# Attention in the first pass: values as weights in two column halves, output by feature, softmax division ahead of the transposes

## The reference, cut to what matters

```python
logits = jnp.where(valid[:, None, :], logits + bias, NEG_INF)
sink = jnp.broadcast_to(sinks.astype(jnp.float32).reshape(1, ATT_KV_HEADS, ATT_GROUP, 1, 1, 1), logits.shape[:-1] + (1,))
probs = jax.nn.softmax(jnp.concatenate([logits, sink], axis=-1), axis=-1)[..., :KEY_BAND]
out = jnp.einsum('bhgcqk,bckhd->bcqhgd', probs, vb)
y = jnp.concatenate([y_rwkv.astype(h.dtype), y_att], axis=-1) @ w_out[l]
```

## Time and profile before

| | |
|---|---|
| median of 3 runs | 2862.46 us (2858.02 to 2865.93) |
| the profiled execution's own time | 2862.2 us |
| its span, first to last instruction | 2860.2 us |
| TensorE matmul / weight load busy | 2483.3 us / 1604.6 us |
| VectorE / ScalarE / GpSimd busy | 1079.2 / 733.6 / 406.3 us |
| mean granted TensorE clock | 0.931 |

### The profile page before, as it was taken

One profiled execution on the slowest core, in us unless ns is written; L12 is line 12 of the kernel. 1 busy time (PEld: TensorE's weight loads), 2 busy tenths in 40 slices (PEclk: granted clock), 3 DMA queues, 4 the chain that ended last, 5 costly groups with the idle time before them and its releaser, 6 DMA issues. The chain is left out here.

```text
span 2860.2 us, 68640 instructions
## 1 busy us (share of the span) xinstructions
PE 2483.3 (87%) x28334; PEld 1604.6 (56%) x28335; DVE 1079.2 (38%) x2622; ACT 733.6 (26%) x1782; POOL 406.3 (14%) x455
## 2 busy tenths in 40 slices
PE   3999999999997699999999995589999999989800
PEld 1888888888886567777777773323333333323200
DVE  0344544545445245656565554211111111111118
ACT  0244343443443113222222221012222222212200
POOL 0212112121121011212121210000000000000013
PEclk7999999999997899999999996599999999999955
DMA  8011121121123823232323210745535679999597
GB/s 318 8 68 66 45 88 47 45 89 45 45 82 121 335 80 108 103 123 83 126 91 113 91 69 37 320 180 220 220 132 220 268 270 362 349 426 358 204 369 284
DMA packets 59767, 472.50 MB, mean 165 GB/s; under 512 B 8284, under 2 KB 9344, under 8 KB 38944
## 3 DMA queue, kind: packets, MB, share of 16 engines
q1 hardware_dynamic: 39432, 403.49, 36.3%
q0 software_dynamic: 9936, 36.18, 3.6%
q10 hardware_dynamic: 10184, 29.67, 2.7%
HBM read 373.90 MB, written 95.42 MB: 164 GB/s over the span
## 5 line engine op out<-in xcount | busy, mean ns | idle before, releaser
L1726 PE MATMUL ps<-arena 128*32 128x512 f32 x4608 | 516.4, 605 | 35.2 <-DMA arena<-wex 35.2
L452 PE MATMUL ps<-arena 128*128 128x128 f32 (+2 forms) x3584 | 419.7, 276 | 2.1 <-ACT arena L601 2.1
L452 PEld LDWEIGHTS ps<-arena 128*128 128x128 f32 (+2 forms) x3584 | 406.9, 186 | 17.0 <-ACT arena L601 13.0
L1726 PEld LDWEIGHTS ps<-arena 128*32 128x32 f32 x4608 | 151.3, 112 | 393.6 <-issue 366.7
L1107 PE MATMUL ps<-arena 64*64 64x64 f32 x8704 | 298.1, 222 | 30.4 <-ACT arena L1310 9.1
L1107 PEld LDWEIGHTS ps<-arena 64*64 64x64 f32 x8704 | 278.0, 136 | 59.1 <-issue 58.0
L1740 PE MATMUL ps<-arena 128*32 128x512 f32 x2304 | 263.8, 598 | 18.1 <-DMA arena<-wex 16.8
L1252 PE MATMUL ps<-arena 128*128 128x512 f32 x512 | 238.9, 610 | 0.7 <-ACT arena L1329 0.7
L1946 DVE TENSOR_TENSOR arena<-arena,ps 128x256 f32<-128x256 f32 x72 | 29.9, 415 | 456.3 <-ACT arena L1785 456.3
L1785 ACT ACT_TABLE_LOAD x36 | 46.2, 1283 | 603.8 <-PE ps L1726 603.8
L463 PE MATMUL ps<-arena 128*128 128x256 f32 (+1 forms) x512 | 174.3, 488 | 0.0
(11 more groups left out here) (321 smaller groups left out, 3033.3 us busy)
## 6 DMA issues: line engine op xcount, KB each, us to landing
arena<-wex SPq DMA_DIRECT2D x108, 2048.0 KB, 9.6
mid<-arena SPq DMA_DIRECT2D x16, 2568.0 KB, 8.5
arena<-mid SPq DMA_DIRECT2D x16, 2568.0 KB, 10.4
arena<-ada SPq DMA_DIRECT2D x12, 2048.0 KB, 11.6
y<-arena ACTq DMA_DIRECT2D x36, 512.0 KB, 8.0
arena<-x SPq DMA_DIRECT2D x31, 512.0 KB, 5.4
arena<-w_in SPq DMA_DIRECT2D x8, 1232.0 KB, 25.6
y<-arena SPq DMA_DIRECT2D x16, 512.0 KB, 11.3
```

What stands on the lines that cost most here:

```text
L452: mm = pe.matmul(bank[name][0:m, at:at + P], V["w_in"][:, kk, w0:w0 + m], V["hT"][:, kk, :], start=(kk == 0), stop=(kk == KD - 1))
L1726: mm = pe.matmul(bank[("HA", "HB")[g]][rows[j], :], xT[:, kk, rows[j]], slot[j][:, at:at + 2 * FH], start=(kk == 0), stop=(kk == KD - 1))
```

## The change

- The step `att5` on TensorE has the values as weights (64 columns) and the transposed probabilities streaming, two heads (256 columns) at a time. The first two heads of a group are written to rows 0 to 63 of C2, the other two to rows 64 to 127: rows are now features. It waits for both halves of `PT` before its first matmul.
- The softmax division moves: VectorE gets a step at the place of `exp_0` and `exp_1` in the order, which waits for `probs`, computes the reciprocal of the sums of 4 heads and multiplies the 4x192 probabilities in place; it signals `pn`, and the transposes wait for that.
- VectorE's `att5_1` is a plain copy of C2 into `ya`.
- In pass 2 the transposes of `ya` are gone; ScalarE copies `ya` straight into `yT` (signal `yaT`), and bank O1 loses its use "yT".
- The rows of `w_out` are reordered ahead of the launch, to match the new order of the attention output.

```diff
--- before.py
+++ after.py
@@ -551,7 +551,7 @@
 
             def att4(g):
                 def go(t, b):
-                    S.wait(pe, "probs", 2 * t + g + 1)
+                    S.wait(pe, "pn", 2 * t + g + 1)
                     for half, name in enumerate(("T0", "T1")):
                         B.wait_free(pe, name, f"P{g}", t)
                         for i in range(2):
@@ -564,12 +564,13 @@
             def att5(g):
                 def go(t, b):
                     B.wait_read(pe, "C2", "gate", t)
-                    for i in range(4):
-                        h = 4 * g + i
-                        B.wait_read(pe, f"T{i // 2}", f"P{g}", t)
-                        for part in range(2):
-                            v = V["qkv"][b if part else 1 - b][:, 640 + 64 * g:704 + 64 * g]
-                            mm = pe.matmul(bank["C2"][:, 64 * h:64 * h + 64], V["PT"][:, i, P * part:P * part + P], v,
+                    for half in range(2):
+                        B.wait_read(pe, f"T{half}", f"P{g}", t)
+                    for part in range(2):
+                        v = V["qkv"][b if part else 1 - b][:, 640 + 64 * g:704 + 64 * g]
+                        for half in range(2):
+                            mm = pe.matmul(split(bank["C2"][64 * half:64 * half + 64, 256 * g:256 * g + 256], 2), v,
+                                           V["PT"][:, 2 * half:2 * half + 2, P * part:P * part + P],
                                            start=(part == 0), stop=(part == 1))
                     mm.then_inc(S["pv"], 1)
                 return go
@@ -860,18 +861,26 @@
                     B.free(dve.tensor_copy(V["PT"][:, 2:4, :], split(bank["T1"][:, :], 2)), "T1")
                 return go
 
+            def probs(g):
+                def go(t, b):
+                    S.wait(dve, "probs", 2 * t + g + 1)
+                    g4 = slice(4 * g, 4 * g + 4)
+                    dve.tensor_tensor(V["den"][:, g4], V["sm"][:, g4], V["es"][:, g4], ALU.add)
+                    dve.drain()
+                    dve.reciprocal(V["den"][:, g4], V["den"][:, g4])
+                    dve.drain()
+                    keys = V["Pm_v"][:, :, 64:256]
+                    dve.tensor_tensor(keys, keys, per_channel(V["den"][:, g4], KEYS), ALU.mult).then_inc(S["pn"], 1)
+                return go
+
             def att5(t, b):
-                S.wait(dve, "probs", 2 * t + 2)
-                dve.tensor_tensor(V["den"], V["sm"], V["es"], ALU.add)
-                dve.drain()
-                dve.reciprocal(V["den"], V["den"])
-                dve.drain()
                 S.wait(dve, "pv", 2 * t + 2)
-                dve.tensor_tensor(split(pk["ya"], QH), split(bank["C2"][:, :], QH), per_channel(V["den"], HD), ALU.mult).then_inc(S["ya"], 1)
+                dve.tensor_copy(pk["ya"], bank["C2"][:, :]).then_inc(S["ya"], 1)
 
             run(dve, {"norm": norm, "ev_r": ev("r"), "ev_k": ev("k"), "ev_v": ev("v"), "ev_lora": ev("lora"),
                       "att1": att1, "kk": kk, "ew1": ew1, "ew2": ew2, "ew3": ew3, "tok1": tok("tokB"), "tok2": tok("tokV"),
-                      "att3_0": att3(0), "att3_1": att3(1), "att4_0": att4(0), "att4_1": att4(1), "att5_1": att5})
+                      "att3_0": att3(0), "att3_1": att3(1), "exp_0": probs(0), "exp_1": probs(1), "att4_0": att4(0),
+                      "att4_1": att4(1), "att5_1": att5})
 
 
 def views(nc, ctx):
@@ -943,7 +952,7 @@
          "X0": ("M", "t0", *(f"x{l}" for l in _LV), "WT"),
          "X1": ("M", "t0", *(f"x{l}" for l in _LV), "WT", "D0", "D1"),
          "YE": ("y",), "YO": ("y",),
-         "O0": ("yT", "o", "hT", "rl"), "O1": ("yT", "o", "hT")}
+         "O0": ("yT", "o", "hT", "rl"), "O1": ("o", "hT")}
 BANK2 = {b: i for i, b in enumerate(("O0", "O1", "Z0", "Z1", "X0", "X1", "YE", "YO"))}
 
 
@@ -1030,6 +1039,7 @@
         def _(sp):
             def load(n, b):
                 B.wait_full(sp, "O0", "yT", n - 2)
+                S.wait(sp, "yaT", n - 1)
                 if not isinstance(n, int) or n >= 2:
                     load_pack(sp, S, W, dram, n, b)
                 if isinstance(n, int) and n == 0:
@@ -1233,13 +1243,11 @@
                 pk = W["pk"][b]
                 if isinstance(t, int) and t == 0:
                     pe.wait_ge(S["mod_added"], MOD1 + MODS)
-                for name, src in (("O1", pk["ya"]), ("O0", W["yc"])):
-                    B.wait_free(pe, name, "yT", t)
-                    if name == "O0":
-                        S.wait(pe, "yr", t + 1)
-                    for c in range(CC):
-                        mm = pe.transpose(bank[name][:, P * c:P * c + P], src[:, P * c:P * c + P], ident)
-                    B.full(mm, name)
+                B.wait_free(pe, "O0", "yT", t)
+                S.wait(pe, "yr", t + 1)
+                for c in range(CC):
+                    mm = pe.transpose(bank["O0"][:, P * c:P * c + P], W["yc"][:, P * c:P * c + P], ident)
+                B.full(mm, "O0")
 
             def o(n0, kk):
                 def go(t, b):
@@ -1247,8 +1255,9 @@
                     if kk == 0:
                         if isinstance(t, int) and t == 0 and n0 == 0:
                             pe.wait_ge(S["w_out"], 32)
-                        for other in ("O0", "O1"):
-                            B.wait_read(pe, other, "yT", t)
+                        B.wait_read(pe, "O0", "yT", t)
+                        S.wait(pe, "yaT", t + 1)
+                        B.wait_free(pe, name, "o", t)
                     mm = pe.matmul(bank[name][:, :], W["yT"][:, kk, :], W["w_out"][:, kk, 512 * n0:512 * n0 + 512],
                                    start=(kk == 0), stop=(kk == KD - 1))
                     if kk == KD - 1:
@@ -1324,9 +1333,11 @@
                 act.activation(W["sqy"], W["yc"], ACT.Square).then_inc(S["sqy"], 1)
 
             def yT(t, b):
-                for i, name in ((1, "O1"), (0, "O0")):
-                    B.wait_full(act, name, "yT", t)
-                    B.free(act.activation(W["yT"][:, 4 * i:4 * i + 4, :], split(bank[name][:, :], 4), ACT.Copy), name)
+                S.wait(act, f"pack{b}", 16 * (t // 2) + 16)
+                B.wait_full(act, "O1", "o", t - 1)
+                act.activation(W["yT"][:, 4:KD, :], split(W["pk"][b]["ya"], 4), ACT.Copy).then_inc(S["yaT"], 1)
+                B.wait_full(act, "O0", "yT", t)
+                B.free(act.activation(W["yT"][:, 0:4, :], split(bank["O0"][:, :], 4), ACT.Copy), "O0")
 
             def norm2(t, b):
                 S.wait(act, "x1", t + 1)
@@ -1372,7 +1383,7 @@
                 pool.tensor_tensor(W["rsy"], W["var"], V["minus_half"][:, 0:8], ALU.pow).then_inc(S["rsy"], 1)
 
             def gn1(t, b):
-                B.wait_full(pool, "O1", "yT", t - 1)
+                B.wait_full(pool, "O0", "yT", t - 1)
                 pool.tensor_tensor(split(W["vb"], H), split(W["pk"][b]["V"], H), per_channel(W["pk"][b]["bon"], HD),
                                    ALU.mult).then_inc(S["vb"], 1)
 
@@ -2058,6 +2069,12 @@
     return np.concatenate([up, down], 1).reshape(NE * PIECES, P, PIECE)
 
 
+def out_rows(w):
+
+    att = w[C:].reshape(KVH, 2, 2, HD, D).transpose(0, 2, 1, 3, 4).reshape(QH * HD, D)
+    return np.concatenate([w[:C], att], 0)
+
+
 def host_arrays(inputs):
 
     a = {n: np.asarray(v) for n, v in inputs.items()}
@@ -2081,7 +2098,7 @@
     return {"x": a["x"].reshape(T, D), "cols": cols, "rows": rows, "consts": consts, "onehot": onehot,
             "gate_b": np.concatenate([b[2], b[5]])[None, :],
             "ada": a["ada_w"][0].reshape(KD, P, 12, 512).transpose(2, 1, 0, 3).reshape(12, P, KD * 512), "w_in": a["w_in"][0], "w2": a["rwkv_w2"][0], "a2": a["rwkv_a2"][0],
-            "g2": a["rwkv_g2"][0], "rel_bias": a["rel_bias"], "w_out": a["w_out"][0],
+            "g2": a["rwkv_g2"][0], "rel_bias": a["rel_bias"], "w_out": out_rows(a["w_out"][0]),
             "w_router": np.concatenate([a["router_grp_w"][0], a["router_exp_w"][0]], 1),
             "wex": expert_pieces(a["exp_w1"][0], a["exp_w3"][0], a["exp_w2"][0])}
```

## The result

The changed kernel takes 2891.94 us (median of 4 runs, 2889.78 to 2894.05) against 2863.15 for the kernel before (4 runs): ratio 1.0103, 95% interval 1.0085 to 1.0120. It is slower by 29 us. The forecast was 2868.5, "same"; the range ended at 2879.

What follows compares the result with a forecast made beforehand. TensorE was taken to bound the kernel, 87% busy. Steady tiles +9.0 us, last tile -1.1 and pass 2 -1.7 sum to +6.2 us, forecast 2868.5 us ("same"), range 2851 to 2879.

Steps and rivals of the forecast that it cites:

- Any new wait of TensorE is paid in full: Pass 1: TensorE works 835 of 852 us at granted clock 0.98, so each added wait costs its own length.
- The chain: Pass 1 softmax work ahead of att5_0: the division makes TensorE start 2.13 us later per tile, waiting 2.4 us.
- The collision: First division in pass 1: VectorE's multiply and GpSimd's subtraction for v cannot read at once, delaying the chain 1.0 us.
- TensorE's saving: Pass 1, two att5 steps per tile: 3.55 us falls to 2.02, saving 1.53 us per tile.
- the seam: TensorE going into and out of 64-column tiles around each att5 step: 0.15 us per step.
- Last tile and pass 2: Last tile of pass 1 saves 1.1 us; pass 2, without four transposes per tile, saves 1.7 us in all.
- The gap of 0.40 us before S0a: Pass 2: after four transposes TensorE waits 0.4 us for VectorE's copy of Z1, leaving 0.11 us saved per tile.
- halves do not run together: Rival at att5: column halves do not overlap, a step takes 1.88 us, total 2896 us; chance 0.06.
- no collision: Rival at the first division: multiply and subtraction run side by side, -0.3 us per tile, 2851 to 2855; chance 0.18.
- pass 2 whole: Rival in pass 2: TensorE not stopped by VectorE's L1415, 7.5 us saved instead of 1.7, total 2863; chance 0.10.

Runs made afterwards that it cites:

- e_nolock: Changed kernel with the first division's multiply replaced by a maximum over the same 768 elements; pass 2 begins at 938.6 us instead of 975.3.
- e_afterhalf: Changed kernel with the loops of att5 exchanged, column half outside and key part inside; 2869.45 us, ratio 1.0025.

## Why the prediction was wrong, point by point

- **"Any new wait of TensorE is paid in full"**: this is the step that failed. The forecast took the granted clock of 0.98 in the earlier trace rows as given and charged the wait once. At 2.25 us the wait also brings the clock to its lower level for about 3.5 us in 12 of 14 periods and behind the 15th wait, at 1.7 us each: the missing term, 20 to 22 us. The forecast's 2868.7 and 22 are 2891, measured 2892. The forecast had in its own rows the sign of it: at the end of pass 1, where TensorE waits, L572 takes 3.65 us instead of 1.89. I used this for the last tile and never asked it of the new wait.
- **The chain**: right in place and nearly in size. Wait 2.25 us against 2.4, releaser VectorE's copy. The collision was real (e_nolock), worth 0.79 instead of 1.0.
- **TensorE's saving**: the step came at 1.02 (forecast 1.01), the tile saved 1.31 to 1.36 instead of 1.53, since the seam is paid outside the step too. The misses here and in the chain cancel, which was luck: (2.25 - 0.30) - 1.36 = +0.59 per tile without a fall, against +0.60.
- **Last tile and pass 2**: from the last xT step to the first matmul of pass 2 it is 106.2 us instead of 104.8. Without the last steady tile's wait (+0.6) and fall (+1.6) that leaves about -0.8 for the last tile, an estimate, against -1.1. The gap of 0.40 us before S0a stands where it was put. Pass 2 took 806.2 to 810.9 us in the nine kernels with the direct copy (mean 808.6) and 811.0 to 812.8 in the four with the transposes (mean 811.8): a gain of about 3 us, of the size of the scatter, where 1.7 was forecast.
- **The rivals**: the rival "halves do not run together" gave 2896 and the measured time is 2892, but its mechanism is refuted by the 1.02 us step. A time that fits proves nothing. The rival "no collision" is refuted by GpSimd's 1.82 us; e_nolock, where the collision is taken away, has a period of 52.3, 0.15 below the kernel before, where that rival had 0.3 per tile. The rival "pass 2 whole" is refuted by the gap of 0.40 us, which ends with VectorE's copy.
- **The verdict bound to the wait**: TensorE waits for both halves of PT ahead of the first matmul. The change's description named it, and the forecast did not price the other choice. Exchanging two loops lets the first half of the step run inside the wait and takes 22 of the 29 us away.

## What to carry to other kernels

When a new wait on TensorE is put into a forecast, price it twice: once as idle time, once as the clock that it may cost, and look in the trace of before for a place where TensorE waited that long and what its matmuls took afterwards. Where a wait can't be removed, let the work that is ready run inside it, even if it goes slower there: in e_afterhalf the halves no longer overlap, and it is 22 us faster. Before adding a step to an engine's queue, look at what stands right behind it and has been ready long since, and at which operation of GpSimd it will meet with two inputs from SBUF.

## What the runs showed that I had not expected

- The fall is steep in the length of the wait and depends on more than that: with the new form of the step none of 14 periods at 1.04, 1.47 (1.8 in three of them) or 1.71 us, twelve at 2.11 and at 2.25; with the old form nine at 1.09 us and about 0.2 inside the step. Two tiles with the same wait can differ, in one execution, by the whole 1.7 us.
- The column halves overlap in either order of issue (step of 1.02 us both ways).
- A GpSimd multiply of 128x768 with a broadcast operand takes 1.48 us against VectorE's 0.96, and costs nothing where VectorE reads PSUM meanwhile. The changed kernel takes 2892 us, with the second division behind the copy 2852, and with the multiplications on GpSimd as well 2841.
